# Projection stage of a hybrid decoder step: operands made straight from a turned copy of the input, the norm's roots applied to the products

## The reference

```python
def rms_norm(x, g):
    y = xf * lax.rsqrt(jnp.mean(xf * xf, axis=-1, keepdims=True) + EPS)
    return (y * g.astype(jnp.float32)).astype(x.dtype)
...
    proj = jnp.einsum('btd,dc->btc', h, w_in)      # h = rms_norm(x, norm1_g)
    qa, ka, va, qk_raw, vb, ob, gates = jnp.split(proj, IN_SPLITS, axis=-1)
...
    conv = b_conv + sum(xp[:, w:w + T] * w_conv[w] for w in range(CONV_W))
    qb, kb = jnp.split(jax.nn.silu(conv), 2, axis=-1)
```

## Time and profile before

| what | value |
|---|---|
| median of 3 runs | 2760.98 us (2754.66 to 2761.34) |
| the profiled execution's own time | 2763.24 us |
| its span in the trace | 2761.4 us |
| mean granted TensorE clock | 0.982 of full |
| transfers | 620.08 MB, mean 225 GB/s |

### The profile page before, as it was taken

The page is one execution under the profiler, slowest core; times in us unless marked ns, Lnnn a source line. Parts: engine busy times, 40 slices in busy tenths (PEclk is TensorE's granted clock), DMA queues, the critical chain, the costliest instruction groups (busy, mean ns, idle before and its releaser), DMA issues. The chain is left out here.

```text
span 2761.4 us, 44514 instructions
## 1 busy us (share of the span) xinstructions
PE 2616.6 (95%) x16803; PEld 2207.9 (80%) x16803; DVE 1783.7 (65%) x3800; ACT 1045.1 (38%) x1927; POOL 689.9 (25%) x585
## 2 busy tenths in 40 slices
PE   7999999999899998679989999899999999999997
PEld 6888888878777776458868888799998888788886
DVE  6722567332688884657667766755655677887778
ACT  4312333010576774223355555555553111221113
POOL 1167212120244543201210000100002443333332
PEclk9999999999999998899999999999999999999999
DMA  5368543254355457966837878778859776887672
GB/s 186 141 209 275 193 150 124 100 208 143 115 168 182 146 166 273 404 255 243 313 128 232 277 270 274 248 264 309 292 196 357 271 252 238 279 295 238 220 260 88
DMA packets 339533, 620.08 MB, mean 225 GB/s; under 512 B 36224, under 2 KB 239172, under 8 KB 325623
## 3 DMA queue, kind: packets, MB, share of 16 engines
q1 hardware_dynamic: 272140, 522.51, 54.6%
q10 hardware_dynamic: 66042, 90.72, 9.0%
q0 software_dynamic: 1152, 4.19, 0.4%
HBM read 446.84 MB, written 237.61 MB: 248 GB/s over the span
## 5 line engine op out<-in xcount | busy, mean ns | idle before, releaser
L3633 DVE TENSOR_TENSOR mlp_acc<-mlp_acc,bank 128x512 f32<-128x512 f32 x440 | 298.7, 684 | 141.5 <-PE bank L2921 137.0
L2919 PE MATMUL bank<-mlp_wd,mlp_u_hi 128*128 128x512 f32 x896 | 350.3, 391 | 8.8 <-DVE mlp_acc L3633 5.0
L2920 PE MATMUL bank<-mlp_wd,mlp_u_hi 128*128 128x512 f32 x896 | 349.4, 390 | 0.0
L2921 PE MATMUL bank<-mlp_wd,mlp_u_lo 128*128 128x512 f32 x896 | 349.4, 390 | 0.0
L3402 ACT ACTIVATE mlp_u_hi<-mlp_u_raw 128x768 fp32r<-128x768 f32 x126 | 113.1, 945 | 445.3 <-POOL mlp_u_raw L3270 444.9
L2919 PE MATMUL bank<-mlp_h_hi,mlp_wu_hi 128*128 128x272 f32 x896 | 259.3, 289 | 9.3 <-DVE mlp_h_lo L3491 4.8
L2920 PE MATMUL bank<-mlp_h_lo,mlp_wu_hi 128*128 128x272 f32 x896 | 258.9, 289 | 0.0
L2921 PE MATMUL bank<-mlp_h_hi,mlp_wu_lo 128*128 128x272 f32 x896 | 257.9, 288 | 0.0
L294 PE MATMUL p_bank<-p_w_hi,p_hT_hi 128*128 128x512 f32 x640 | 250.4, 391 | 5.6 <-DVE p_stage L838 5.6
L296 PE MATMUL p_bank<-p_w_hi,p_hT_lo 128*128 128x512 f32 x640 | 249.1, 389 | 0.0
L295 PE MATMUL p_bank<-p_w_lo,p_hT_hi 128*128 128x512 f32 x640 | 249.0, 389 | 0.0
(11 more groups left out here) (455 smaller groups left out, 5943.0 us busy)
## 6 DMA issues: line engine op xcount, KB each, us to landing
mlp_wd<-wd SPq DMA_DIRECT2D x31, 2048.0 KB, 8.0
mlp_wd<-wd SPq DMA_DIRECT2D x32, 1536.0 KB, 7.6
mlp_u_raw<-u SPq DMA_DIRECT2D x256, 128.0 KB, 2.4
out_win_k_sample<-in_cache_k SPq DMA_DIRECT2D x48, 680.0 KB, 9.0
out_win_v_sample<-in_cache_v SPq DMA_DIRECT2D x48, 680.0 KB, 8.9
mlp_wu_raw<-in_w_up SPq DMA_DIRECT2D x31, 1024.0 KB, 6.3
p_w_raw<-in_w_tok SPq DMA_DIRECT2D x10, 2048.0 KB, 10.0
wd<-mlp_un_hi SPq DMA_DIRECT2D x21, 896.0 KB, 4.5
```

Of the source, the lines that this page charges most:

```text
L2919: nc.tensor.matmul(out, ah, bh, start=fresh and k == 0, stop=False, skip_group_check=not fresh)
L2920: nc.tensor.matmul(out, ah, bl, start=False, stop=False, skip_group_check=not fresh)
L2921: ins = nc.tensor.matmul(out, al, bh, start=False, stop=k == n - 1, skip_group_check=not fresh)
L3633: v.tensor_tensor(a, a, b[:], ALU.add).then_inc(summed, 1)
```

## The change

The host lays the input out a second time, turned (`x_t`, width on partitions), and the gain as one number per partition and block. `Columns` makes the operands from it: for g = 0 in two pieces of 512 tokens, block by block of the width (`act_piece`, `dve_piece`), for g = 1 tile by tile (`act_tile`, `dve_tile`). They carry the gain but not the root, and the turns of the input by TensorE are gone.

The roots are made beside this by `Roots`, from the rows of `x`: ScalarE squares all 17 tiles, in three batches of 4, 4 and 9 tiles. Where the product has tokens on the partitions (`tile_out`) the root is a scalar per partition of the same VectorE instructions. Where tokens are columns (chunks and gates) the roots are needed along the columns in every partition: TensorE turns each tile's root, repeated 128 times (`spread`), into PSUM, ScalarE copies it to `rbc`, and VectorE multiplies it in when it reads the products out. So `evac` moves from ScalarE to VectorE, and ScalarE keeps the margins (`heads`); the first part of a chunk is now read out inside the convolution of the chunk before. For g = 0 chunk 1 goes to the spare banks 6 and 7. The gates take four VectorE instructions per part in place of two.

```diff
+    PIECE, PIECES = 512, 2
...
+    def load_piece(self, sp, p, q):
+        k = slice(2 * q, 2 * q + 2)
+        sp.dma_start(self.pieces[p][:, k], self.x_t[:, k, p * self.PIECE:(p + 1) * self.PIECE]).then_inc(self.piece_in[p][q], 16)
+    def load_tile(self, sp, n):
+        if n >= 2:
+            sp.wait_ge(self.lo_ready, self.HEAD + n - 1)
+        T = 8 + n
+        sp.dma_start(self.tiles[:, n % 2], self.x_t[:, :, T * P:(T + 1) * P]).then_inc(self.tile_in[n % 2], 16)
+    def act_piece(self, act, p):
+        at = slice(p * self.PIECE, (p + 1) * self.PIECE)
         for k in range(KC):
...
+            if k % 2 == 0:
+                act.wait_ge(self.piece_in[p][k // 2], 16)
+            self.nc.scalar.activation(self.hi[:, k, at], self.pieces[p][:, k], ACT.Copy,
+                                      scale=self.gain[:, k:k + 1]).then_inc(self.hi_ready, 1)
...
+    def dve_piece(self, dve, p):
+        at = slice(p * self.PIECE, (p + 1) * self.PIECE)
+        for k in range(KC):
+            dve.wait_ge(self.hi_ready, KC * p + k + 1)
+            self.nc.vector.scalar_tensor_tensor(self.lo[:, k, at], self.pieces[p][:, k], self.gain[:, k:k + 1],
+                                                self.hi[:, k, at].bitcast(F32), ALU.mult, ALU.subtract).then_inc(self.lo_ready, 1)
+    def act_tile(self, act, n, w):
+        act.wait_ge(self.tile_in[n % 2], 16 * (n // 2) + 16)
+        for k in range(KC):
+            last = self.nc.scalar.activation(self.hi[:, k, n * P:n * P + w], self.tiles[:, n % 2, k, 0:w], ACT.Copy,
+                                             scale=self.gain[:, k:k + 1])
         last.then_inc(self.hi_ready, 1)
...
+    def dve_tile(self, dve, n, w, beside=False):
+        dve.wait_ge(self.hi_ready, self.HEAD + n + 1)
+        for k in range(KC):
+            hi = self.hi[:, k, n * P:n * P + w]
+            for dst in (self.lo[:, k, n * P:n * P + w], self.hi[:, k, n * P + w:n * P + 2 * w])[0:2 if beside else 1]:
+                last = self.nc.vector.scalar_tensor_tensor(dst, self.tiles[:, n % 2, k, 0:w], self.gain[:, k:k + 1],
+                                                           hi.bitcast(F32), ALU.mult, ALU.subtract)
         last.then_inc(self.lo_ready, 1)
...
+    def square(self, act, T):
+        act.wait_ge(self.row_in[T], 16)
+        self.nc.scalar.activation(self.homes[T], self.homes[T], ACT.Square, accum_out=self.q[:, 0, T:T + 1]).then_inc(self.ssq, 1)
...
+        late = [xb[:, 0]] + [front(f"row{n}", at, [P, D])[:] for n, at in
+                             enumerate((W + D, W + 2 * D, W + 3 * D, 2 * W + D, 2 * W + 2 * D, 2 * W + 3 * D, 3 * D))]
+        roots = Roots(nc, sem, lambda T: xv[T],
+                      [xn[:, 0], xn[:, 1], acc[:, 1, 0:D], raw[:, 0, 0:D], raw[:, 1, 0:D]] + late + late[0:4], stats)
...
                 load_first()
+                sp.dma_start(gain[:], K.norm1_g).then_inc(gain_in, 16)
+                for q in range(4):
+                    cols.load_piece(sp, 0, q)
+                sp.dma_start(wg_raw[:], K.w_gate).then_inc(wg_in, 16)
+                for q in range(4):
+                    cols.load_piece(sp, 1, q)
+                sp.wait_ge(hi_ready, 1)
+                sp.dma_start(wq_raw, K.w_qk[1]).then_inc(wq_in, 16)
                 sp.dma_start(st24, K.state_conv).then_inc(state_in, 16)
-                sp.dma_start(wg_raw[:], K.w_gate).then_inc(wg_in, 16)
-                for T in (4, 5, 6, 7):
-                    norm.head_load(sp, T)
+                for T in range(6):
+                    roots.load(sp, T)
+                sp.wait_ge(cols.lo_ready, KC)
+                for T in (6, 7):
+                    roots.load(sp, T)
...
+                roots.load(sp, 8)
+                sp.wait_ge(cols.lo_ready, 2 * KC)
+                for T in range(9, 13):
+                    roots.load(sp, T)
...
                             sp.wait_ge(lo_ready, 13)
                             load_first()
                 base = 13 * g
-                sp.wait_ge(norm.xn_ready, 16 if g else 2)
-                sp.dma_start(wq_raw, K.w_qk[1]).then_inc(wq_in, 16)
+                if g:
+                    sp.wait_ge(cols.lo_ready, cols.HEAD + 8)
+                    sp.dma_start(wq_raw, K.w_qk[1]).then_inc(wq_in, 16)
                 for c in range(2, 8):
                     sp.wait_ge(lo_ready, c + base)
                     sp.dma_start(wq_raw, K.w_qk[c]).then_inc(wq_in, 16)
-                    if c == 2:
+                    if g == 0 and c == 2:
+                        for T in range(13, TILES):
+                            sp.wait_ge(roots.ssq, T - 7)
+                            roots.load(sp, T)
+                    if c == 3 - g:
...
-                    norm.act_head(act, lambda: round_first(0), head_gates)
-                    act.wait_ge(act_state, 1)
-                    act.wait_ge(tail_zero, 1)
-                    round_chunk(0, 1, 1)
-                if g:
+                    round_first(0)
+                    act.wait_ge(gain_in, 16)
+                    cols.act_piece(act, 0)
+                    head_gates()
+                    cols.act_piece(act, 1)
+                    head_state()
+                    for T in range(4):
+                        roots.square(act, T)
+                    roots.act_root(act, 0)
+                    round_chunk(0, 1, 1, (cols.lo_ready, KC))
+                    spread(0, 0, 512)
+                    for T in range(4, 8):
+                        roots.square(act, T)
+                    roots.act_root(act, 1)
+                    round_chunk(0, 2, 0, (qk_mm, n))
+                    for T in range(8, 13):
+                        roots.square(act, T)
+                    spread(1, 1, 512)
+                    store_gates(0)
+                    act.wait_ge(roots.ssq, 5)
+                    heads(0, 0, 0, False)
+                    heads(0, 1, 1, False)
+                    for T in range(13, TILES):
+                        roots.square(act, T)
+                    squash(0, 0, 0)
+                    store(0, 0, 0)
+                else:
                     act.wait_ge(un_out[0], 32 * SET.count(0))
-                evac(g, 0, 0, 0, g > 0)
-                evac(g, 0, 0, 1)
...
+            def evac(g, c, j, q, source):
+                at, w = GC[g][q], min(GW[g][q], SPLIT - GC[g][q])
+                dve.wait_ge(qk_mm, QB[g] + NPC[g] * c + q + 1)
+                ins = v.tensor_tensor(raw[:, j, 3 + at:3 + at + w], source[:, 0:w], rbc[:, at:at + w], ALU.mult)
+                if q == 2:
+                    ins = v.tensor_tensor(sraw[:, j, :, 3:3 + DEC_T], source[:, w:w + NS].rearrange("p (b t) -> p b t", b=DEC_B),
+                                          rbc[:, SPLIT:SPLIT + NS].rearrange("p (b t) -> p b t", b=DEC_B), ALU.mult)
+                ins.then_inc(qk_out, 1)
+            def conv(g, c, j, stored, between=None, last=False, spare=False):
+                for q in range(1, NPC[g]):
+                    evac(g, c, j, q, bank[6 + q if spare else q])
+                dve.wait_ge(headed, 8 * g + c + 1)
                 dve.wait_ge(qk_out, QB[g] + NPC[g] * (c + 1))
                 if stored is not None:
                     dve.wait_ge(acc_out[j], 16 * stored)
...
+                if not last:
+                    if not isinstance(c, int) or g or c:
+                        dve.wait_ge(conv_out, 8 * g + c)
+                    evac(g, c + 1, 1 - j, 0, bank[6 if g == 0 and isinstance(c, int) and c == 0 else 0])
...
+                chain.link(v.tensor_scalar(stage[:, slot], bank[2 + s][:], r, None, ALU.mult))
...
-                    chain.link(v.tensor_scalar(stage[0:8, q, 0:w], bank[GB[q]][0:8, 0:w], bg[:, 0:1], None, ALU.add))
-                    v.tensor_tensor(stage[0:8, q, 0:w], stage[0:8, q, 0:w], bank[GB[q]][LO_AT:LO_AT + 8, 0:w],
-                                    ALU.add).then_inc(gate_ready, 1)
+                    dve.wait_ge(rb_ready, q + 1 if g == 0 else 5)
+                    at = GC[g][q]
+                    chain.link(v.tensor_copy(stage[0:8, q, 0:w], bank[GB[q]][0:8, 0:w]))
+                    chain.link(v.tensor_tensor(stage[0:8, q, 0:w], stage[0:8, q, 0:w], bank[GB[q]][LO_AT:LO_AT + 8, 0:w], ALU.add))
+                    chain.link(v.tensor_tensor(stage[0:8, q, 0:w], stage[0:8, q, 0:w], rbc[0:8, at:at + w], ALU.mult))
+                    v.tensor_scalar(stage[0:8, q, 0:w], stage[0:8, q, 0:w], bg[:, 0:1], None, ALU.add).then_inc(gate_ready, 1)
...
+                    if g == 0 and t:
+                        cols.dve_tile(dve, t - 1, P)
...
-                    norm.dve_lo_beside(dve, 2 * n, 0, n * P, NS)
+                    cols.dve_tile(dve, 7, P)
+                    cols.dve_tile(dve, 8, NS, beside=True)
...
+            def spread(q, tiles):
+                for n, T in enumerate(tiles):
+                    last = nc.tensor.transpose(bank[(4, 5, 7)[q]][:, n * P:(n + 1) * P], roots.of(T).broadcast_to([P, P]), ident[:])
+                return last
...
```

(23 more changed lines are left out.)

362 lines of the change are left out of this document (108 added, 254 removed).

## The result

The changed kernel took 2767.34 us (median of 14 runs, 2762.19 to 2771.92), the kernel before 2759.28 us beside it (14 runs, 2754.66 to 2765.41): a ratio of 1.0031, with a 95% interval of 1.0022 to 1.0039. It is 8.1 us slower, where I had forecast 10.2 us faster. The profiled execution has a span of 2765.4 us.

A forecast was written before the change was run, and what follows sets the result against it. TensorE, busy 95% of the span, was taken as the bound. 3.7 + 0.5 + 7.8 + 1.2 - 1.0 - 2.0 = 10.2 us gained, so the median 2760.98 becomes 2750.8; 8-in-10 range 2743 to 2760.

The forecast's parts named there:

- What bounds the kernel: Whole kernel: TensorE is busy for 95% of the span, so gains come where it waits or makes no product.
- the head: Projection's start: chunk 2 begins 5.4 us earlier, less 1.7 for the lower clock: 3.7 us gained, bounds -4 and 8.
- The chunk loops: Both halves: TensorE stays the bound by 0.3 to 0.5 us a chunk; a shorter wait before token tiles gains 0.5.
- I cost that at nothing: Token tiles' output: the root as a further scalar costs nothing, covered by VectorE's slack in each 5.4 us tile.
- Turns in the second half: Second half: removed turns gain 7.8 us, row waits 1.2; spread turns cost 1.0; tile preparation hidden but for tenths.
- The last two tiles: Second half's start: preparing tiles 7 and 8 late, with GpSimd holding VectorE, loses 2.0 us, bounds 0 and 4.
- the rivals: Slow queue, chance 0.12; VectorE bounding the loops, 2755.5, 0.17; head gives nothing, 2754.5, 0.13; head gives more, 2746, 0.15.
- a slow queue in the head: Head: at 285 GB/s the 13.3 MB land at 51, 13 us later, kernel about 2764; chance 0.12.

The follow-up runs named there:

- experiment 4: Changed kernel with the norm's root left out of the token-major tile outputs, which use the earlier kernel's instructions: 2761.97 us, ratio 1.0007 to the kernel before.
- experiment 1: Changed kernel with ScalarE preparing each second-half tile before storing the token product's output, in the first half's last token block: 2754.79 us, ratio 0.9981.
- experiment 2: Changed kernel with each second-half tile prepared by one 1024-column instruction per engine instead of eight of 128, gain left out: 2753.28 us, ratio 0.997.
- experiment 6: Changed kernel with a filler, 48 idle products of 512 columns, in TensorE's pause before chunk 2: 2768.38 us, ratio 1.0024.
- the combined ones: Changed kernel with three ScalarE order edits together, 2745.30 us; plus a weaker chunk 2 wait, 2748.34; or plus moved copies, 2738.44; those with 26 filler products, 2738.97.

## Why the prediction was wrong, by its own steps

- **What bounds the kernel, and the head:** right in mechanism, a size too good. Chunk 2 gained 3.95 where I had 5.4 (the weights came 1.9 later, and the convolution started 1.6 later); the clock cost 1.9, read as the filler's gain, where I had 1.7. Head: 2.05, not 3.7, and that from one execution on each side: in the seven kernels with this head chunk 2 started between 55.8 and 56.8, in the two with the head before at 59.0 and 59.7.
- **The chunk loops:** right. The intervals are 10.88 and 11.86. Of the two waits of 1.7 that I meant to shorten by 0.5, the one at the second half's tokens fell from 1.66 to 0.64; the one at the third block of the first half grew by 0.24. I had put both down to ScalarE's readings, but the second is the whole output of the tile before (experiment 4).
- **"I cost that at nothing"** (the root in the tile output): 0.24 at that wait, and behind it the clock fell for eight products, 1.6 us. That is the 1.8 between 213 and 302, together with the spread turns (0.9 for nine, as forecast) less 0.7 for a wait near 290 that went. The two hang together. In six of the kernels with the root in the output the clock fell here, and near 290 TensorE waited 0.1 at the most; in five it did not fall, and there the wait was 0.1 to 1.2. From the one wait to the last token block the six took 89.7 to 90.1 us and the five 88.5 to 89.6, so the 1.6 came to about half a microsecond in the mean.
- **Turns in the second half, the step that failed:** "they end some 6 us after it, and the next tile output has 5.4 us: hidden but for tenths, since the banks are two". I scaled the eight instructions to 1.5 and 1.7 us from longer ones; they take 2.45 and 2.19. And I compared a delay with an interval, but did not close the ring: the store at whose issue ScalarE waits stands behind VectorE's output, and the next preparation behind the store. Closed with my own sizes, and the 0.43 that the issue takes, the round would have been 1.5 + 1.7 + 1.5 for the output + 0.43 = 5.1 us, still under the tile's 5.45. So it is the mis-sized term that failed, by 1.4 us, with 0.25 more from the output; the ring is why that size mattered. Banks help against a late instruction, not against a round that is longer than the tile. From the block's start to the half's first product before took 52.3 us, experiment 1 takes 43.6 and the changed kernel 47.8: 8.7 us of turns and row waits went, and only 4.5 arrived; the gates' wait of 2.4 is the ring's last round.
- **The last two tiles:** I had the chain right (tile 7, load, rounding, tile 8) and priced it at 2.0 with a hold by GpSimd. But it came late as a whole: the weights' load was issued at +13.1 (362.74, against the half's first product at 349.67) where I had +5.2, since tile 7 began only behind the ring's last round, at +8.4, and took 4.6 us of both engines where I had 3.2. The load was quicker than I had it, 3.5 us to the rounding in place of 5.1. ScalarE's eight short instructions for tile 8 took 2.00 where I had 0.9, VectorE's sixteen 3.5 where I had 2.1, and the hold by GpSimd met only the first of them (0.56 in place of 0.27). TensorE, itself 2.4 late by the gates' wait, had other products until +16.6. The wait was 6.52, and the lower clock behind it cost another 2.1. From the half's first product to chunk 1 the changed kernel took 31.0 us and experiment 1 21.7, with waits of 0.9 and 0.6 left, against 20.7 before.
- **What I had not seen:** the burst of copies, 2.7. The sum had no term for the second half's token tiles; there the stores land late, and what TensorE waits depends on which tiles meet the burst.

The Trainium skill's page VectorE: DVE Perf Modes, in the section The TRN2 errata, states that instructions on ScalarE and VectorE which read SBUF pay a fixed extra latency each, so that many small tiles pay it many times. The trace agrees: ScalarE's 128 columns took 0.31 us (2.45 for eight) and its 64 columns 0.25 (2.00 for eight), while one instruction of 1024 took 1.06. By the page's formula, 224 cycles and one for each column at 1.2 GHz, eight of 128 columns are an estimated 2.35 us. With that estimate in place of my 1.5 the round in my own sizes would have been 6.0 us, over the tile's 5.45.

None of the rivals was this one. The slower side that I had named (a slow queue in the head) was measured wrong: the weights landed at 39.9, not at 51.

## What to carry to other kernels

When work is moved between tiles, write down the closed round (who waits for whom until the same instruction comes again) and compare its sum with the bounding engine's interval; two idle engines beside a waiting third are the sign of a ring. Price short instructions by a row of their own length, never by scaling a long one. And where a stretch holds a burst of transfers, try the kernel with the burst spread out as well, before you put a few microseconds down to your change.

## What the runs showed of the hardware

- Whether the clock falls behind a wait is not set by its length alone. Eleven of the kernels here waited 1.9 us at the third token block; in six (the changed one, experiments 1, 2 and 6, and two of the combined ones) the first three to five products came at full rate and the seven or eight behind them 0.427 us apart (the changed kernel's granted clock was 0.50 from 213.5 to 216), in five all came at full rate. Behind the wait of 1.65, in the three kernels without the root in the output, the clock did not fall; three are too few to say that the 0.24 made the difference. In experiment 1 a wait of 2.7 near 560 had no such products behind it. Behind the head's pauses of 5.9 to 12.4 us products came at the lower rate in each of the ten kernels without a filler, and in neither with one: there, standing still is the cause.
- A VectorE instruction with one source in SBUF (TENSOR_SCALAR, 8x512) took 2.51 us in place of 0.47 beside GpSimd's split, in each of the five kernels with the changed head, and ended 0.27 or 0.28 us after GpSimd's instruction each time. I had expected that of two-source instructions only. The Trainium skill's page SBUF — State Buffer, in its section SBUF: two separate sides, names VectorE's two-port fast modes beside the instructions with two SBUF inputs as those that GpSimd locks out; the rows agree with it as far as they go, but do not show the mode.
